# A pooling mixer rebuilt as projection first and banded products on TensorE, and the last expert routing table left in SBUF

## The chip, the cores and the metric

The kernel runs on one core of a Trainium2 chip. The metric is the device time of one execution in microseconds. The kernel before takes 3367.31 us, the median of three runs (3367.08 to 3372.91).

## What is computed

A residual block with depth 2 and then a second block, on 512 tokens (T) of 1024 channels (D), all in float32. Order of the work: feed-forward 0, pooling mixer, feed-forward 1 (layer 0); feed-forward 2, convolution mixer, feed-forward 3 (layer 1); then a mixer of attention and a linear recurrence, and a product-key expert layer (PEER) with 16384 single-neuron experts. The two parts that the change touches:

```python
def pool_mixer(h, w_grp, scale):          # windows 2, 4, 8, 16, one for each group of 256 channels
    cs = cumsum(hg, axis=1)
    pooled = (cs - lag(cs, w)) / min(pos, w)
    mixed = pooled - hg
    return einsum('btgc,gcd->btgd', mixed, w_grp) * scale

def peer_ffn(x, ...):                     # per token, 8 heads x 16 picks
    g = softmax(best_s); u = expert_u[idx]; v = expert_v[idx]
    return einsum('thk,thkd->td', g * gelu(einsum('td,thkd->thk', xc, u)), v)
```

The h that enters the pooling mixer is `x * rstd * coef + shift`, with rstd the inverse root of the mean square of a token over its channels, and coef and shift per channel from the conditioning vector c.

## The kernel before, in words

**Layout.** Activations are held transposed: channels on the 128 partitions, the 512 tokens along the free axis, in 8 tiles `x[:, k, :]` of 128x512. Every product is made in split precision: each operand is written as a high part (fp32r, made by ScalarE) and a low part (the rest, made by VectorE or GpSimd), and three matmuls (high by high, high by low, low by high) go into one PSUM bank (`three`, L1763).

**Weight stream.** One stream of 599 groups of 128x1024 weights (512 KB each) goes through a ring of R = 4 slots. SyncE loads a group into `raw` (L505) when the low part of the group four before is made; ScalarE makes `whi` (`hi`, L567 to L575) when TensorE has used the slot; GpSimd makes `wlo` (L532), and in the last two stages VectorE does (L1601). A semaphore carries each of these steps. All instructions of an engine are issued in the order of the program, so a waiting instruction holds up what stands behind it on its engine.

**Around the pooling mixer.** The output product of feed-forward 0 ends in four banks; VectorE adds each to x (L1262), ScalarE squares the tile (L594), VectorE sums the squares (L1096), and `mean_square` (L1836) takes the mean over the channels with a matmul by a constant matrix, so that each partition has the mean square of every token. Then come a root on ScalarE (L612) and a reciprocal of 128x512 on VectorE (`inverse_root`, L1113). The mixer itself, before: for each of 8 tiles VectorE multiplies by rstd (L1335), ScalarE applies scale and shift into a padded row (L701), VectorE makes the window sum by 1, 2, 3 or 4 shifted additions (`pool_mix`, L1314), corrects the first tokens (L1319), divides and subtracts (L1320), ScalarE makes the high part (L707), VectorE the low part (L1328), and only then can TensorE multiply by the group's weights: 48 matmuls of 512 columns (issued through `three`). VectorE adds the results to x (L1344). Eight `keep_busy` matmuls stand at the head of this stage on TensorE.

**Next stage.** Feed-forward 1 starts with `deferred_pair` (L1801): its first two weight groups are multiplied by `x * coef` not yet normed (`xs_hi` by `scaled_high`, L603; `xs_lo` by `scaled_low`, L1126), the norm is put on the result afterwards. Before, it first waits for the seventh tile of x; L1819 is its first matmul. `first_pair` (L1780) does groups three and four with the normed h.

**Expert layer, first pass ("up").** For each of 128 columns m of experts TensorE makes 24 matmuls of 384 columns (tokens 128 to 511), ScalarE applies gelu and stores the result (192 KB) to DRAM `expert_acts` (L930). Tokens 0 to 127 are done by gathered rows instead: GpSimd issues 128 indirect DMAs of 512 KB into a ring of 4 (L556), and VectorE takes a dot product of each (L1613). In between, 16 chunks for each of three blocks of 128 tokens (j = 0, 1, 2) are turned into a routing table `spread` (64 KB in each partition) by one-hot matmuls (L2142). After the chunks of a block its table is written to DRAM `expert_weights` in 8 pieces of 1 MB (L994) during the columns that follow: for j = 2 one piece per column from column 112 on. After these ScalarE issues the load of x back from DRAM (`x_back`, 2 MB, L998).

**Expert layer, second pass ("down").** For each m ScalarE loads one column of the tables (`g_ring`, 192 KB, L1013) and the stored gelu (`act_in`, 192 KB, L1014), three columns ahead; VectorE multiplies them (L1723), ScalarE makes the high part (L1025), VectorE the low part (L1727), and TensorE makes 18 matmuls of 512 columns (L2183 to L2185). For each m VectorE also adds one gathered row of v to the result of the first 128 tokens (L1735). VectorE still has nine dot products and four low parts of weights to make in order before and between the first of these steps. Before step 3 ScalarE waits until all gelu results are stored. After step 3 TensorE turns x_back by 64 small matmuls (L2165) and goes on.

## Time and profile before

| | before |
|---|---|
| median of 3 runs | 3367.31 us |
| profiled execution | 3378.14 us |
| its span | 3376.3 us |
| mean granted TensorE clock | 0.973 |
| TensorE matmul busy | 3223.0 us, 95% |
| VectorE busy | 2039.0 us, 60% |
| ScalarE busy | 1319.1 us, 39% |
| GpSimd busy | 1371.8 us, 41% |
| DMA | 636.91 MB |

The profile is one execution taken by the hardware profiler. Shares over the whole span say little for a change to two places; the sections of the span in which TensorE is not full are where time can be won. A granted clock of 1 is the level of 2.4 GHz, 0.5 that of 1.2 GHz. Times in brackets in a row of the time line are the idle time of the engine just before, with what ended it.

### The profile page before, as it was taken

Reading aid. Unit: us, or ns where it says so; the run is one execution under the profiler, and the core shown is the slowest. Engines: PE = TensorE matmul, PEld = TensorE weight load, DVE = VectorE, ACT = ScalarE, POOL = GpSimd, SP = SyncE. Lnnn points to the kernel's source line nnn. Section 1 sums busy time; section 2 is a strip of 40 time slices with the busy share of each in tenths; the row PEclk is TensorE's granted clock in tenths of the full one; section 3 lists DMA queues with packets and bytes.
Section 4 is the critical chain, followed back from the end, with each engine's and each line's share of the span. In section 5 each row is a group of like instructions: output and inputs, shape, how many; then the busy total and the mean of one; then the engine's idle time right before and its main releaser. Section 6 shows DMA issues by size and latency. Waiting matters only on the chain. (4 is left out here: it accounts for less than half of the span.)

```text
span 3376.3 us, 44805 instructions
## 1 busy us (share of the span) xinstructions
PE 3223.0 (95%) x15268; PEld 2753.7 (82%) x15268; DVE 2039.0 (60%) x2980; ACT 1319.1 (39%) x2029; POOL 1371.8 (41%) x686
## 2 busy tenths in 40 slices
PE   6999889999999999999998899999989897999999
PEld 4888668888888888888876677999989896888887
DVE  5562386613653164411157668987957766888887
ACT  3222243323332233322244653244857652333333
POOL 3444335444544444444443224466423343222221
PEclk8999989999999999999999889999999998999999
DMA  6554325532654222222322003355888899999997
GB/s 251 195 189 144 106 88 205 195 110 81 216 191 145 95 89 99 94 93 95 106 81 75 25 32 113 102 172 172 293 322 306 291 349 363 342 361 361 366 358 273
DMA packets 237531, 636.91 MB, mean 189 GB/s; under 512 B 22880, under 2 KB 105056, under 8 KB 233824
## 3 DMA queue, kind: packets, MB, share of 16 engines
q1 hardware_dynamic: 89440, 324.78, 27.5%
q10 hardware_dynamic: 111104, 176.30, 14.8%
q0 software_dynamic: 36864, 134.23, 11.2%
q8 instruction: 72, 1.18, 0.1%
q14 instruction: 51, 0.42, 0.0%
HBM read 580.69 MB, written 54.53 MB: 188 GB/s over the span
## 5 line engine op out<-in xcount | busy, mean ns | idle before, releaser
L532 POOL TENSOR_TENSOR wlo<-raw,whi 128x1024 fp32r<-128x1024 f32 x394 | 1022.4, 2598 | 1233.3 <-ACT whi L575 1232.7
L1765 PE MATMUL bank<-hhi,whi 128*128 128x512 f32 (+1 forms) x2688 | 1005.8, 374 | 51.4 <-DVE hlo L1328 22.1
L1766 PE MATMUL bank<-hlo,whi 128*128 128x512 f32 (+1 forms) x2688 | 997.2, 371 | 0.0
L1767 PE MATMUL bank<-hhi,wlo 128*128 128x512 f32 (+1 forms) x2688 | 996.6, 371 | 0.0
L575 ACT ACTIVATE whi<-raw 128x1024 fp32r<-128x1024 f32 x599 | 631.9, 1058 | 911.2 <-PE bank L1767 532.9
L1765 PEld LDWEIGHTS bank<-hhi,whi 128*128 128x128 f32 x2688 | 510.0, 190 | 123.8 <-issue 23.9
L1767 PEld LDWEIGHTS bank<-hhi,wlo 128*128 128x128 f32 x2688 | 509.4, 190 | 66.8
L1766 PEld LDWEIGHTS bank<-hlo,whi 128*128 128x128 f32 x2688 | 510.0, 190 | 66.1 <-issue 0.7
L1064 DVE CUSTOM_DVE_ANT_0 ada_raw<-ada_raw,cond_row 128x1024 f32<-128x1024 f32 x128 | 307.3, 2432 | 156.9 <-DMA ada_raw<-ada_dram 156.8
L1601 DVE TENSOR_TENSOR wlo<-raw,whi 128x1024 fp32r<-128x1024 f32 x205 | 250.7, 1223 | 161.8 <-ACT whi L575 140.2
L2183 PE MATMUL bank<-whi,we 128*128 128x512 f32 x768 | 300.4, 391 | 9.4 <-DVE we L1727 6.1
L556 POOL DMA_INDIRECT ring<-u_rows_dram,cell_u x128 | 179.2, 1400 | 298.0 <-DVE dots L1613 278.7
L2184 PE MATMUL bank<-whi,we 128*128 128x512 f32 x768 | 299.9, 390 | 0.0
L2185 PE MATMUL bank<-wlo,we 128*128 128x512 f32 x768 | 299.7, 390 | 0.0
L556 POOL DMA_INDIRECT ring<-stream_dram,cell_v x128 | 140.9, 1101 | 365.1 <-DVE y L1735 354.9
L1765 PE MATMUL bank<-uhi,whi 128*128 (+1 forms) x704 | 273.9, 389 | 0.0
L1766 PE MATMUL bank<-ulo,whi 128*128 (+1 forms) x704 | 273.9, 389 | 0.0
L1767 PE MATMUL bank<-uhi,wlo 128*128 (+1 forms) x704 | 273.9, 389 | 0.0
L644 ACT ACTIVATE uhi<-u 128x512 f32 (+1 forms) x88 | 55.6, 632 | 421.7 <-DVE u L1207 419.1
L1207 DVE TENSOR_TENSOR u<-silu,bank 128x512 f32<-128x512 f32 x85 | 58.2, 685 | 260.1 <-PE bank L1767 215.6
L2183 PEld LDWEIGHTS bank<-whi,we 128*128 128x128 f32 x768 | 144.8, 189 | 40.7 <-issue 4.9
L1613 DVE CUSTOM_DVE_ANT_0 ring<-ring,h_row 128x1024 f32<-128x1024 f32 x128 | 153.2, 1220 | 36.8 <-DMA ring<-u_rows_dram,cell_u 36.6
(326 smaller groups left out, 4063.6 us busy)
## 6 DMA issues: line engine op xcount, KB each, us to landing
raw<-stream_dram SPq DMA_DIRECT2D x599, 512.0 KB
ada_raw<-ada_dram ACTq DMA_DIRECT2D x128, 512.0 KB, 4.1
expert_acts<-act_out ACTq DMA_DIRECT2D x128, 192.0 KB
expert_weights<-spread ACTq DMA_DIRECT2D x24, 1024.0 KB
g_ring<-expert_weights ACTq DMA_DIRECT2D x128, 192.0 KB
act_in<-expert_acts ACTq DMA_DIRECT2D x128, 192.0 KB
first_raw<-ada_dram SPq DMA_DIRECT2D x8, 1024.0 KB, 18.1
x<-xin_dram ACTq DMA_DIRECT2D x1, 2048.0 KB, 7.1
```

The source lines that it names most:

```text
L532: pool.tensor_tensor(wlo[:, s, :, :], raw[:, s, :, :], whi[:, s, :, :].bitcast(F32), ALU.subtract).then_inc(lo_ready, 1)
L556: pool.indirect_dma_start(ring[:, q % RING, :], None, rows, bass.IndirectOffsetOnAxis(ap=cell[:, c:c + 1], axis=0)).then_inc(ring_landed[q ...
L575: act.activation(whi[:, s, :, :], raw[:, s, :, :], ACT.Copy).then_inc(hi_ready, 1)
L1064: dve.tensor_tensor_reduce(ada_raw[:, u % 2, :], ada_raw[:, u % 2, :], cond_row[:, :], 1.0, 0.0, ALU.mult, ALU.add, ada_dot[:, u % KT:u % ...
L1601: dve.tensor_tensor(wlo[:, s, :, :], raw[:, s, :, :], whi[:, s, :, :].bitcast(F32), ALU.subtract).then_inc(lo_ready, 1)
L1613: dve.tensor_tensor_reduce(ring[:, q % RING, :], ring[:, q % RING, :], h_row[:, :], 1.0, 0.0, ALU.mult, ALU.add, dots[:, q:q + 1]).then_in ...
L1765: pe.matmul(bank, whi[:, s, b, :], rhi, start=start, stop=False)
L1766: pe.matmul(bank, whi[:, s, b, :], rlo, start=False, stop=False)
L1767: return pe.matmul(bank, wlo[:, s, b, :], rhi, start=False, stop=stop)
L2183: pe.matmul(bank, we[:, m % WSLOTS, 0, toks], rh, start=m == 0, stop=False, skip_group_check=True)
L2184: pe.matmul(bank, we[:, m % WSLOTS, 1, toks], rh, start=False, stop=False, skip_group_check=True)
L2185: mm = pe.matmul(bank, we[:, m % WSLOTS, 0, toks], rl, start=False, stop=last, skip_group_check=True)
```

## The change

**Pooling mixer.** The mean over tokens and the multiplication by the group weights commute, and the factor rstd of a token can be put on after the weights. The new kernel multiplies `xs = x * coef` (made as for the deferred pairs, `scaled_high(1, k)` and `scaled_low(1, k)`, the first four tiles during feed-forward 0) by the weights with xs stationary and the weights moving, so that the result z has tokens on the partitions: `project`, 6 matmuls of 256 columns for each of 4 token tiles and 4 groups. The same product for the shift (`wide`, 24 matmuls) is made first and copied to SBUF by ScalarE. The mean square is made per token on a partition (four matmuls of two columns), so root and reciprocal are of 128x8. VectorE makes z = psum * rstd + wide_out (8 of 128x512), ScalarE rounds (8), VectorE makes the low parts (8). Pooling minus identity is then a product of z with constant banded matrices, 144 columns wide, 8 matmuls for each of 8 channel tiles and one more for the first tokens of windows 4, 8 and 16. The result lands in channel layout and VectorE adds it to x as before. The constants (576 KB) are loaded on ScalarE's queue during the output product of feed-forward 0; `pool_setup` and one rounding of 128x1152 on ScalarE prepare them there. `keep_busy(8)`, the padded rows and the DMA of `corr` go. The deferred pair of feed-forward 1 waits for the fourth tile of x instead of the seventh.

**Expert layer.** The table of block j = 2 stays in `spread` and is no longer written out or read back: `g_ring` loads shrink to 128 KB, VectorE's multiplication is two instructions (256 and 128 columns), and the wait for the last written pieces goes. Buffers move: `x_back` now lies where hhi was and is loaded after the last up column, ahead of the last store of `expert_acts` on the same queue.

The diff, cut to what the text speaks of:

```diff
...
+    bands_raw = place("bands_raw", 88, [P, 4, 2 * BAND], F32)
+    bands = place("bands", 187.5, [P, 4, 2 * BAND], F32R)
+    wide_hi = place("wide_hi", 195.5, [P, KT, P], F32R)
+    wide_lo = place("wide_lo", 199.5, [P, KT, P], F32R)
+    wide_out = place("wide_out", 139.5, [P, D], F32)
+    z32 = place("z32", 175.5, [P, 4, T], F32)
+    z_hi = place("z_hi", 107.5, [P, TT, D], F32R)
+    z_lo = place("z_lo", 123.5, [P, TT, D], F32R)
...
-    we = place("we", 100, [P, WSLOTS, 2, TD], F32R)
-    x_back = place("x_back", 116, [P, KT, T], F32)
-    y = place("y", 132, [P, TT, D], F32)
-
-
-    expert_weights = nc.dram_tensor("expert_weights", (DT, P, NK, P), F32).ap()
+    act_in = place("act_in", 181, [P, 4, TD], F32)
+    we32 = place("we32", 187, [P, 2, TD], F32)
+
+    we = [place(f"we{s}", at_kb, [P, 2, TD], F32R) for s, at_kb in enumerate((190, 193, 196, 172))]
+    x_back = place("x_back", 64, [P, KT, T], F32)
+    y = place("y", 80, [P, TT, D], F32)
...
+    expert_weights = nc.dram_tensor("expert_weights", (DT - 1, P, NK, P), F32).ap()
...
                     if q == 0:
                         for k in range(4):
                             ada_load(KT * LATE + 4 * half + k)
+                        if half == 0:
+                            act.dma_start(bands_raw[:, :, :], bands_in).then_inc(const_landed, 16)
+                        else:
+                            act.wait_ge(const_landed, 64)
+                            act.wait_ge(u_ready, FT)
+                            act.activation(bands[:, :, :], bands_raw[:, :, :], ACT.Copy).then_inc(bands_hi, 1)
                     with act.Fori(0, 2) as i:
                         for j in range(4):
                             hi(c + 1 + j, i, 4)
                     if half:
                         for k in range(4):
                             square(SUB_NORM[q] + 1, k)
-                            if q:
-                                scaled_high(7 if q == 3 else SUB_NORM[q] + 1, k)
+                            scaled_high(7 if q == 3 else SUB_NORM[q] + 1, k)
...
-            norm(1, pool_out, squared=4)
-            pool_round(KT - 1)
+            for k in range(4, KT):
+                square(1, k)
+                scaled_high(1, k)
+            act.wait_ge(pool_banks, 1)
+            for half in range(2):
+                act.activation(wide_out[:, half * T:(half + 1) * T], psum[6 + half][:, :], ACT.Copy).then_inc(wide_copied, 1)
+            act.wait_ge(ms_ready, ALL_NORMS.index(1))
+            act.activation(tok_std[:, :], psum[3][:, 0:2 * TT], ACT.Sqrt, bias=S("eps")).then_inc(std_ready, 1)
             hi(SEG["pool"][0] + LOOK)
-            hi(SEG["pool"][0] + LOOK + 1)
+            for half in range(2):
+                for tt in range(TT):
+                    act.wait_ge(pool_z, TT * half + tt + 1)
+                    act.activation(z_hi[:, tt, half * T:(half + 1) * T], z32[:, tt, :], ACT.Copy).then_inc(pool_hi, 1)
+                if half == 0:
+                    hi(SEG["pool"][0] + LOOK + 1)
             norm(2, h_high, ahead=SEG["ffn1_in"][0] + LOOK)
...
-                    pieces = (k,) if j == DT - 1 else (2 * k, 2 * k + 1)
-                    for p in pieces:
-                        if p < PIECES:
+                    for p in (2 * k, 2 * k + 1):
+                        if j < DT - 1 and p < PIECES:
                             rows = slice(PIECE * p, PIECE * p + PIECE)
-                            act.dma_start(expert_weights[j][:, rows, :], spread[:, rows, :]).then_inc(
-                                spilled if j < DT - 1 or p < PIECES // 2 else spilled_late, 16)
-                    if j == DT - 1 and k == PIECES:
-                        act.wait_ge(spilled, 16 * PIECES * (DT - 1) + 16 * PIECES // 2)
-                        act.dma_start(x_back[:, :, :], x_kept).then_inc(x_landed, 16)
+                            act.dma_start(expert_weights[j][:, rows, :], spread[:, rows, :]).then_inc(spilled, 16)
                     column(CHUNK_AT[j] + CHUNKS + k, None)
...
+            act.dma_start(x_back[:, :, :], x_kept).then_inc(x_landed, 16)
             store_acts(NK - 1, None)
             act.wait_ge(ring_used, PICKS)
             act.activation(gel[:, :], dots[:, :], ACT.Gelu_apprx_tanh).then_inc(gel_ready, 1)
-            act.wait_ge(spilled_late, 16 * PIECES // 2)
...
+            def pool_setup():
+
+                dve.wait_ge(bands_hi, 1)
+                for g in range(1, 4):
+                    w = 2 << g
+                    dve.tensor_tensor(corner_lo[:, CORNER[w]:CORNER[w] + w], bands_raw[:, g, 0:w], bands[:, g, 0:w].bitcast(F32),
+                                      ALU.subtract).then_inc(setup_done, 1)
+                shift = mod[:, 3 * KT:4 * KT].unsqueeze(2).to_broadcast([P, KT, P])
+                dve.wait_ge(ada_used, KT * (LATE + 1))
+                dve.tensor_copy(wide_hi[:, :, :], shift).then_inc(setup_done, 1)
+                dve.wait_ge(setup_done, 5)
+                dve.tensor_tensor(wide_lo[:, :, :], shift, wide_hi[:, :, :].bitcast(F32), ALU.subtract).then_inc(setup_done, 1)
...
+            def pool_low(q):
+                half, tt = q // TT, q % TT
+                dve.wait_ge(pool_hi, q + 1)
+                cols = slice(half * T, (half + 1) * T)
+                dve.tensor_tensor(z_lo[:, tt, cols], z32[:, tt, :], z_hi[:, tt, cols].bitcast(F32), ALU.subtract).then_inc(pool_ready, 1)
+
+            dve.wait_ge(std_ready, ALL_NORMS.index(1) + 1)
+            dve.reciprocal(tok_rstd[:, :], tok_std[:, :]).then_inc(rstd_ready, 1)
+            dve.wait_ge(rstd_ready, ALL_NORMS.index(1) + 1)
+            dve.wait_ge(wide_copied, 2)
+            for q in range(2 * TT):
+                half, tt = q // TT, q % TT
+                if tt < TT - 1:
+                    dve.wait_ge(pool_banks, 3 * half + tt + 2)
+                else:
+                    dve.wait_ge(pe_groups, SEG["pool"][0] + half + 1)
+                if q >= TT:
+                    dve.wait_ge(pool_ready, q - TT + 1)
+                dve.scalar_tensor_tensor(z32[:, tt, :], psum[4 - 4 * half + tt][:, :], tok_rstd[:, 2 * tt:2 * tt + 1],
+                                         wide_out[:, half * T:(half + 1) * T], ALU.mult, ALU.add).then_inc(pool_z, 1)
+                if q:
+                    pool_low(q - 1)
+            pool_low(2 * TT - 1)
+            for k in range(KT):
                 dve.wait_ge(pool_mixed, k + 1)
-                dve.tensor_tensor(hlo[:, k, :], mix32[:, k % 2, :], hhi[:, k, :].bitcast(F32), ALU.subtract).then_inc(pool_ready, 1)
-
-            inverse_root(1)
-            for k in range(KT + 1):
-                if k < KT:
-                    if k >= 2:
-                        dve.wait_ge(pool_h, k - 1)
-                    dve.tensor_tensor(xn[:, k % 2, :], x[:, k, :], rstd[:, :], ALU.mult).then_inc(xn_ready, 1)
-                if k:
-                    pool_mix(k - 1)
-            pool_low(KT - 1)
-            for k in range(KT):
-                if k % 4 == 3:
-                    dve.wait_ge(pe_groups, SEG["pool"][0] + k // 4 + 1)
-                else:
-                    dve.wait_ge(pool_banks, 3 * (k // 4) + k % 4 + 1)
-                dve.scalar_tensor_tensor(x[:, k, :], psum[k][:, :], coef[:, 1, KT + k:KT + k + 1], x[:, k, :],
+                dve.scalar_tensor_tensor(x[:, k, :], psum[(k + 4) % KT][:, :], coef[:, 1, KT + k:KT + k + 1], x[:, k, :],
                                          ALU.mult, ALU.add).then_inc(x_ready, 1)
...
-                dve.tensor_tensor(we32[:, m % 2, :], act_in[:, m % 4, :], g_ring[:, m % 4, :], ALU.mult).then_inc(we_mul, 1)
+                dve.tensor_tensor(we32[:, m % 2, 0:TD - P], act_in[:, m % 4, 0:TD - P], g_ring[:, m % 4, :], ALU.mult)
+                dve.tensor_tensor(we32[:, m % 2, TD - P:TD], act_in[:, m % 4, TD - P:TD], spread[:, m, :], ALU.mult).then_inc(we_mul, 1)
...
-                pe.wait_ge(x_ready, KT * (min(n, 8) - 1 - (n == 7)) + (7 if n in (2, 5, 10) else 4))
+                pe.wait_ge(x_ready, KT * (min(n, 8) - 1 - (n == 7)) + (7 if n in (5, 10) else 4))
...
-            keep_busy(8)
-            mean_square(1)
...
+            def project(out, g, hi, lo):
+
+                rows = pool_weights(g)
+                for k in range(2):
+                    pe.matmul(out, hi(2 * g + k), rows[k][0], start=k == 0, stop=False, skip_group_check=True)
+                    pe.matmul(out, hi(2 * g + k), rows[k][1], start=False, stop=False, skip_group_check=True)
+                for k in range(2):
+                    mm = pe.matmul(out, lo(2 * g + k), rows[k][0], start=False, stop=k == 1, skip_group_check=True)
+                return mm
+
+            pe.wait_ge(lo_ready, pool0 + 2)
+            pe.wait_ge(setup_done, 6)
+            pe.wait_ge(x_ready, 4)
             for g in range(4):
-                c = SEG["pool"][0] + g // 2
-                if g % 2 == 0:
-                    pe.wait_ge(lo_ready, c + 1)
-                pe.wait_ge(pool_ready, 2 * g + 2)
-                for o in range(2):
-                    for k in range(2):
-                        mm = three(psum[2 * g + o][:, :], c % R, (g % 2) * 4 + o * 2 + k, hhi[:, 2 * g + k, :], hlo[:, 2 * g + k, :],
-                                   k == 0, k == 1)
-                    mm.then_inc(pe_groups if g % 2 and o else pool_banks, 1)
+                mm = project(psum[6 + g // 2][:, 256 * (g % 2):256 * (g % 2) + 256], g,
+                             lambda k: wide_hi[:, k, :], lambda k: wide_lo[:, k, :])
+            mm.then_inc(pool_banks, 1)
+            for half in range(2):
+                pe.wait_ge(xs_hi_ready, scaled_before(1) + 4 * half + 4)
+                pe.wait_ge(xs_ready, scaled_before(1) + 4 * half + 4)
+                for tt in range(TT):
+                    if half == 0 and tt == 2:
+                        pe.wait_ge(wide_copied, 2)
+                        pe.wait_ge(sq_used, tiles_before(SQ_NORMS, 1) + KT)
+                        for m in range(TT):
+                            mm = pe.matmul(psum[3][:, 2 * m:2 * m + 2], sqsum[:, P * m:P * m + P], mean_d[:, 0:2], start=True, stop=True,
+                                           skip_group_check=True)
+                        mm.then_inc(ms_ready, 1)
+                    if half and tt == 3:
+                        pe.wait_ge(std_ready, ALL_NORMS.index(1) + 1)
+                    for g in (2 * half, 2 * half + 1):
+                        mm = project(psum[4 - 4 * half + tt][:, 256 * (g % 2):256 * (g % 2) + 256], g,
+                                     lambda k: xs_hi[1][:, k, P * tt:P * tt + P], lambda k: xs_lo[1][:, k, P * tt:P * tt + P])
+                    mm.then_inc(pool_banks if tt < TT - 1 else pe_groups, 1)
+            for half in range(2):
+                pe.wait_ge(pool_ready, TT * half + TT)
+                for k in range(4 * half, 4 * half + 4):
+                    g, w = k // 2, 2 << (k // 2)
+                    out, cols = psum[(k + 4) % KT], slice(P * k, P * k + P)
+                    for part in (z_hi, z_lo):
+                        first = part is z_hi
+                        for tt in range(TT):
+                            n = min(BAND, T - P * tt)
+                            at_col = 0 if tt == 0 else BAND
+                            mm = pe.matmul(out[:, P * tt:P * tt + n], part[:, tt, cols], bands[:, g, at_col:at_col + n],
+                                           start=first and tt == 0, stop=not first and tt == TT - 1, skip_group_check=True)
+                        if first and g:
+                            pe.matmul(out[:, 0:w], z_hi[:, 0, cols], corner_lo[:, CORNER[w]:CORNER[w] + w], start=False, stop=False, skip_group_check=True)
+                    mm.then_inc(pool_mixed, 1)
             ffn(1, KT)
...
```

## Rows read from the trace of the kernel before

**Rows 1.** The page: the span and each engine's busy time, share and instructions.
```profile
span 3376.3 us, 44805 instructions
...
PE 3223.0 (95%) x15268; PEld 2753.7 (82%) x15268; DVE 2039.0 (60%) x2980; ACT 1319.1 (39%) x2029; POOL 1371.8 (41%) x686
```

**Rows 2.** Windows: us, busy time of each engine, PEclk, DMA share, GB/s.
```profile
404.00:454.00 50.00, 21.16 (x67) 15.40 (x66) 46.38 (x76) 23.37 (x34) 4.92 (x2) 0.70 0.08 27
454.00:483.00 29.00, 29.00 (x133) 23.97 (x134) 24.61 (x35) 13.33 (x19) 8.17 (x2) 0.93 0.11 37
2739.00:2835.00 96.00, 74.47 (x388) 72.26 (x387) 54.95 (x79) 24.34 (x33) 39.01 (x31) 0.91 1.02 404
2835.00:2866.00 31.00, 26.20 (x133) 21.73 (x132) 21.43 (x33) 11.18 (x18) 6.98 (x5) 0.85 0.93 315
2866.00:3372.00 506.00, 506.00 (x2237) 419.07 (x2236) 413.70 (x489) 191.41 (x242) 135.62 (x124) 1.00 0.96 342
```

**Rows 3.** Time line of PE around the pooling mixer: start us, us, what.
```profile
403.42 0.39 PE L1767 MATMUL bank<-uhi,wlo 128*128 128x512 f32 x1
...
438.55 0.76 PE L1765 MATMUL bank<-hhi,whi 128*128 128x512 f32 x1 [6.23 <-DVE hlo L1328]
...
453.86 0.77 PE L1819 MATMUL bank<-xs_hi,whi 128*128 128x512 f32 x1 [6.72 <-issue]
```

**Rows 4.** Time line of DVE in the same stretch.
```profile
408.69 3.35 DVE L1113 RECIPROCAL rstd<-std 128x512 f32<-128x512 f32 x1 [1.49 <-ACT std L612]
...
443.47 1.40 DVE L1344 SCALAR_TENSOR_TENSOR x<-bank,coef,x 128x512 f32<-128x512 f32 x2
...
447.12 2.19 DVE L1096 TENSOR_TENSOR sqsum<-sqsum,sq 128x512 f32<-128x512 f32 x1
...
449.90 0.67 DVE L1096 TENSOR_TENSOR sqsum<-sqsum,sq 128x512 f32<-128x512 f32 x1
```

**Rows 5.** Time line of PE: matmuls of 256 columns in the attention stage.
```profile
1922.21 0.28 PE L2025 MATMUL bank<-w_lo,v_hi 128*128 128x256 f32 x1
1922.33 0.29 PE L2026 MATMUL bank<-w_hi,v_lo 128*128 128x256 f32 x1
```

**Rows 6.** Time line of PE: matmuls of 128 columns in the query stage.
```profile
2160.40 0.28 PE L2093 MATMUL bank<-key_hi,qt_hi 128*128 128x128 f32 x1
2160.51 0.27 PE L2094 MATMUL bank<-key_lo,qt_hi 128*128 128x128 f32 x1
```

**Rows 7.** Time line of PE at the turn from up to down.
```profile
2834.63 0.77 PE L2183 MATMUL bank<-whi,we 128*128 128x512 f32 x1 [4.61 <-DVE we L1727]
...
2840.79 0.79 PE L2183 MATMUL bank<-whi,we 128*128 128x512 f32 x1 [3.26 <-ACT act_out L938]
...
2855.10 0.47 PE L2183 MATMUL bank<-whi,we 128*128 128x512 f32 x1 [1.54 <-DVE we L1727]
```

**Rows 8.** DMA from 2739 to 2835 us: totals and issues by line.
```profile
DMA packets 12154, 38.79 MB, mean 404 GB/s; under 512 B 1235, under 2 KB 5204, under 8 KB 10998
...
expert_weights<-spread ACTq DMA_DIRECT2D x8, 1024.0 KB
...
x_back<-x_kept ACTq DMA_DIRECT2D x1, 2048.0 KB, 27.0
...
ring<-u_rows_dram,cell_u POOLq DMA_INDIRECT x31
```

**Rows 9.** The page: DMA issues, KB each, us to landing.
```profile
x<-xin_dram ACTq DMA_DIRECT2D x1, 2048.0 KB, 7.1
```

**Rows 10.** Time line of ACT: the wait for the stored gelu results.
```profile
2852.17 1.06 ACT L575 ACTIVATE whi<-raw 128x1024 fp32r<-128x1024 f32 x1 [5.35 <-DMA expert_acts<-act_out]
```

**Rows 11.** Time line of DVE: one step of the down pass, and act_w.
```profile
2854.87 0.28 DVE L1747 TENSOR_TENSOR act_w<-gel,gain 128x128 f32<-128x128 f32 x1
...
3201.04 0.55 DVE L1723 TENSOR_TENSOR we<-act_in,g_ring 128x384 f32<-128x384 f32 x1
3202.31 1.23 DVE L1601 TENSOR_TENSOR wlo<-raw,whi 128x1024 fp32r<-128x1024 f32 x1 [0.72 <-ACT whi L575]
```

129 lines of the change are left out of this document (49 added, 80 removed).

## Prediction

> **What bounds the kernel now.** I read the page first: TensorE (PE) is busy 95% of a span of 3376.3 us [rows 1], so only places where PE stands still or runs at the lower clock can give time. The windows show them [rows 2]. From 2866 to 3372 us, the down pass, PE is full at clock 1.00: 505.9 us for 124 steps, 4.08 us each. Nothing there can be won on another engine. Two places are not full. Around the pooling mixer, from the last matmul of feed-forward 0 at 403.42 to the first of feed-forward 1 at 453.86, 50.4 us pass [rows 3], PE is busy for under half of that and its clock averages well below 1 [rows 2]; the time line says that PE waits for VectorE (DVE), 6.23 us in the gap shown [rows 3], while DVE makes window sums without a pause. And from 2739 to 2866 us, the end of the up pass, PE is busy 74.5 of 96 us and 26.2 of 31 us, with the DMA engines at a share of 1.02 and 0.93 [rows 2]: there the bound is the transfers. 404 GB/s is what they reach with this mix [rows 8].
>
> **Pooling mixer, step by step.** The time line is redone from 403.65 us, when PE is free.
> PE, projections: 24 matmuls for the shift and 4 x 4 x 6 = 96 for xs, all of 256 columns. The nearest rows put such a matmul 0.12 us after the one before [rows 5], so 120 x 0.12 = 14.4 us, and about 0.9 us for the four mean-square matmuls of two columns (eight passes at the 0.11 us at which matmuls of 128 columns follow each other [rows 6]). PE ends its projections at 419.0. xs of tiles 0 to 3 is made 10 us earlier, beside the output product; the four more passes of ACT over a tile there push one weight rounding by under 3 us, which the ring of four slots covers; if it did not, PE would lose those 3 us.
> DVE and ACT beside it: squares are summed by about 406, xs_lo of the last four tiles by 408.6, wide_out is copied by 408.2 (two ACT copies of about 0.6 us after the first 24 matmuls end at 406.5), the mean square is there at about 410.1, root and reciprocal are now of eight columns, some 0.6 us together instead of 3.35 us for the reciprocal alone [rows 4]. From 410.8 DVE makes eight times z (0.66 us, as two readings of a bank took 1.40 in [rows 4]) and its low part (0.6 us, as the 0.67 us addition there): 10.1 us, to about 421. In it falls GpSimd's making of two weight low parts; beside such a piece of work one addition of two SBUF tiles took 2.19 us instead of 0.67 [rows 4], so I add 1.5 us for each: 424. The bound below is no such loss, 421.
> The Trainium skill says of this ("GPSIMD Engine Reference", Key points) that GpSimd shares its SBUF interfaces with VectorE and contends with instructions that have two SBUF inputs. By that the low parts are hit and the z, with one input in PSUM, are not, and the trace agrees: 2.19 against 0.67 us.
> PE, bands: 8 x 8 matmuls of at most 144 columns and 6 corners, 70 x 0.112 = 7.8 us. The first half can run at once from 419.0 to 422.8; the second waits for DVE at 424 and ends at 428.
> DVE then needs 1.26 us per tile of x (0.66 and 0.6 for the sum of squares), so the fourth tile is there at about 428.2, and the deferred pair, which no longer waits for the seventh, starts there. That is 25.7 us before 453.86 [rows 3].
> After that: before, the window from 454 to 483 ran at a mean clock of 0.93 [rows 2], which is 29 x 0.07 = 2.0 us; with PE not idle for more than about 2 us at a time it should start at full clock. Against this stands the mean square in the middle of the deferred pair, which needs all eight tiles: PE gets there at about 434, the last sum at 434.8, 0.9 us. Gain of this part: 25.7 + 2.2 - 0.9 = 27 us. Its ends: 30 (no contention at all) and 20 (each hand-over between PE, ACT and DVE 0.3 us dearer over some 24 of them).
> For narrow matmuls the Trainium skill ("TensorE: Matmul & The Clock Gate", Back-to-back issue gap) gives 81 ns as the sustained spacing at 128 columns. The trace has 0.11 us here, weight load included [rows 6], and the sum goes by that; by the page's figure the bands would take 5.7 us instead of 7.8, an estimate, most of it hidden behind DVE.
>
> **Start.** One small DMA less stands ahead of the weight loads on SyncE: between 0 and 0.5 us, taken as 0.3.
>
> **Expert table, up pass.** Removed between 2739 and 2835 us: eight writes of 1 MB, 8.39 MB, the load of x back, 2.10 MB, and 64 KB of each of five loads of the tables, 0.33 MB: 10.8 of 38.8 MB [rows 8]. The 28.0 MB that stay need 69 us at 404 GB/s. PE alone needs 16 columns x 24 matmuls x 0.1735 us = 66.6 us. DVE needs 36 gathered rows in this stretch; 31 came in 96 us before, 3.1 us each [rows 8], beside the large writes. The queues do not interlock perfectly, since DVE takes rows and weights in one order, so I take 76 to 77 instead of 69 us: 96 - 77 = 19 us won. Ends: 26 (only the bytes count) and 10 (the gathers stay at 2.4 us each, 36 x 2.4 = 86).
>
> **Expert table, turn to down.** What was hidden before is now in the way: x_back is issued only after the last up column, and the last store of the gelu results stands behind its 2 MB on the same queue. ACT waits for that store before step 3, and with it wait the rounding and low part of the weights of step 3 and all later loads of tables. Before, that wait was 5.35 us [rows 10] and cost PE 1.54 us [rows 7]. A load of the same size took 7.1 us at the start of the kernel [rows 9] and 27.0 us when it came behind the writes [rows 8]. In the new place little else is in its queue, so it is nearest to 7.1 to 9 us: the store lands 4 to 7 us later, PE waits 5 us more. Ends: 2 and 20 us. PE itself needs x_back only after 16.3 us of its own steps.
> The Trainium skill ("DMA: Bandwidth & Descriptors", Queues, rings and completion order) says that a DMA engine goes round between queues by packets and takes one ring in order. By that the store cannot pass x_back, which is the cost just named; no row of before shows that order.
>
> **Down pass.** DVE's one multiplication of 0.55 us [rows 11] becomes one of 256 and one of 128 columns, about 0.42 and 0.28 us (the latter as act_w [rows 11]); issued back to back they cost some 0.07 to 0.15 us more. DVE stands idle 0.72 us in each step [rows 11], so that hides them and the cost is nothing; without that idle time it would be 124 x 0.1 = 12 us. Table loads of 128 instead of 192 KB free DMA time that PE does not wait for: 0.
>
> **Sum.** 27 + 0.3 + 19 - 5 = 41.3 us. The profiled execution took 3378.14 us, 10.8 more than the median of 3367.31. Against its own time: 3336.8. Taken from the median: 3326.0 us, if the parts are as large without the profiler. The 10.8 us may well lie in the stretch that is bound by DMA; then its gain is smaller in the timed runs by up to that.
>
> **Rivals.**
> (a) The turn eats the second part: x_back is slow again, near the 27.0 us of [rows 8]; the store comes 20 us late, and the 19 us are given back, or the gathers stay the bound and little was won. For it: share 1.02 in the stretch [rows 2] and four gathers in flight at the turn. Against it: the 8 MB that stood before it in its queue are gone. Time: 3367.3 - 27 = 3340.
> (b) The change does not do on PE what it says: the projections run at the lower clock, 1.2 GHz, at which 256 columns take 0.213 us, as [rows 3] show 6.23 us gaps before a slow start, and DVE's chain, not PE, sets the pace with each hand-over. 120 x (0.213 - 0.12) = 11 us less: 3337. Against it: PE is full from 403.65 on, and the gaps foreseen are under 2 us.
> The Trainium skill ("TensorE: Matmul & The Clock Gate", HAM oscillation) warns of thin matmuls with waits between them, after which the clock falls again and again; by that this rival is the outcome. The waits on the trace that went with a fall here are of 6 us and more [rows 3].
> (c) Both parts reach their upper ends, 30 and 26 - 2: 3313.
> (d) Slower than before: in the down pass the pair of multiplications costs more than the row it replaces plus DVE's idle time, 0.47 + 0.72 = 1.19 us per step; from there each 0.1 us costs 124 x 0.1 = 12.4 us, and it needs 1.6 us a step to make the kernel slower by 7 us (41 + 7 = 48 us over 124 steps). For it: two instructions in place of one and the contention of [rows 4], where one took 1.5 us more. Against it: GpSimd computes nothing there. Time: 3375.
>
> **How the numbers follow.** Forecast 0.58, (a) 0.19, (b) 0.12, (c) 0.07, (d) 0.04. The forecast's case spans 3316 to 3337 by the bounds of its terms; with (a) and (b) and the doubt over the profiler's 10.8 us the range is 3314 to 3345. A measurement of this kernel can tell some 0.2%, 6.7 us, from no change. All cases but (d) are faster by more; I leave 0.01 for no change.
>
> **What would show it.** PE's first matmul of the deferred pair about 25 us after the last of feed-forward 0, instead of 50.4, with the granted clock 1.00 through the stage; z starting at about 411 and ending at 421 to 424; PE with at most two waits of 1 to 2 us. The first matmul of the down pass 77 us after the last chunk (96 before), no issue to expert_weights for the third block, x_back landing in 7 to 10 us, and a PE wait of 5 to 8 us before step 3. The forecast is wrong if PE shows waits in the steady down pass, if the clock falls between 404 and 430, or if the stretch from 2739 stays above 86 us.

## The result and the profile after

The changed kernel takes 3338.1 us (median of 4 runs, 3336.3 to 3339.6); the kernel before, run beside it and earlier, 3368.7 us. The ratio is 0.9896, 95% interval 0.9884 to 0.9908. So the change gives 30.6 us, where 41.3 were forecast, and the time is 12.1 us above the forecast of 3326.0. 3338.1 lies in the range of 3314 to 3345, but just outside the 3316 to 3337 that the terms of the sum allowed by themselves. The profiled execution took 3338.93 us, with a span of 3337.1 us, 39.2 less than the span of before [rows 1]. So the two traces differ by 8.6 us more than the medians do, and part of what is laid out below is a difference between executions.

The windows of after, at the stages of [rows 2] (us, busy time of each engine with the number of instructions, granted clock, DMA share, GB/s):

```profile
412.00:420.00 8.00, 8.00 (x71) 8.00 (x69) 8.00 (x10) 3.36 (x5) 3.24 (x2) 1.00 0.22 68
420.00:428.00 8.00, 6.25 (x37) 6.12 (x36) 7.82 (x13) 5.30 (x10) 0.00 (x0) 0.65 0.18 66
428.00:436.00 8.00, 8.00 (x30) 7.13 (x30) 7.89 (x13) 5.39 (x9) 0.00 (x0) 0.50 0.01 2
...
2709.00:2787.00 78.00, 68.15 (x389) 67.00 (x388) 54.65 (x80) 24.02 (x33) 40.88 (x31) 0.98 0.97 362
2787.00:2827.00 40.00, 29.48 (x134) 24.09 (x134) 21.89 (x41) 11.38 (x18) 6.53 (x5) 0.78 0.85 294
2827.00:3337.00 510.00, 506.37 (x2236) 419.01 (x2235) 422.25 (x609) 191.96 (x243) 143.28 (x124) 1.00 0.92 326
```

PE (TensorE) is full from 404 to 420 us and again from 428, where before it was busy 21 of 50 us. But the clock falls in the window from 420 to 428 us (0.65) and is 0.50 in the next. The up-pass stretch is 78 us long instead of 96; the turn behind it is longer, 40 us instead of 31, with a clock of 0.78 instead of 0.85; the down pass is as full as before but for the last 4 us of the span.

The time line of PE around the pooling mixer, which answers to [rows 3] (last matmul of feed-forward 0, first band product, the second half of the bands, first matmul of the deferred pair, first matmul on hhi):

```profile
402.16 0.39 PE L1763 MATMUL bank<-uhi,wlo 128*128 128x512 f32 x1
...
417.67 0.56 PE L1949 MATMUL bank<-bands,z_hi 128*128 128x144 f32 x4
...
423.32 1.12 PE L1949 MATMUL bank<-bands,z_hi 128*128 128x144 f32 x4 [1.75 <-DVE z_lo L1317]
...
431.06 0.73 PE L1815 MATMUL bank<-xs_hi,whi 128*128 128x512 f32 x1
...
448.91 0.48 PE L1783 MATMUL bank<-hhi,whi 128*128 128x512 f32 x1
```

The deferred pair starts 28.9 us after feed-forward 0, against 50.4 before. There is one wait of 1.75 us, for DVE's last low parts. In front of it 32 band products and two corners took 3.9 us (417.67 to the wait's begin at 421.57, 0.11 us each); behind it 32 and four take 7.7 us (423.32 to 431.06, 0.21 each).

DVE and GpSimd in the same stretch, which answers to [rows 4]:

```profile
407.77 0.17 DVE L1122 CAST shifts<-mod 128x8 fp32r<-128x8 f32 x1
...
409.67 1.41 DVE L1331 SCALAR_TENSOR_TENSOR z<-bank,tok_rstd,wide_out 128x512 f32<-128x512 f32 x2
...
410.42 2.41 POOL L537 TENSOR_TENSOR wlo<-raw,whi 128x1024 fp32r<-128x1024 f32 x1 [9.67 <-ACT whi L580]
...
411.12 2.25 DVE L1317 TENSOR_TENSOR z_lo<-z,z_hi 128x512 fp32r<-128x512 f32 x1
...
413.96 0.68 DVE L1317 TENSOR_TENSOR z_lo<-z,z_hi 128x512 fp32r<-128x512 f32 x1
...
417.74 2.21 DVE L1317 TENSOR_TENSOR z_lo<-z,z_hi 128x512 fp32r<-128x512 f32 x1
...
423.18 1.40 DVE L1338 SCALAR_TENSOR_TENSOR x<-bank,coef,x 128x512 f32<-128x512 f32 x2
...
440.94 3.35 DVE L1116 RECIPROCAL rstd<-std 128x512 f32<-128x512 f32 x1 [2.09 <-ACT std L617]
```

The first row is a cast of eight columns, to be met again below. The long reciprocal is gone, z starts at 409.67, and the two low parts that meet GpSimd's work take 2.25 and 2.21 us, the others 0.68. Then DVE goes on to the x updates without a pause; it stands idle 2.09 us ahead of the reciprocal of the next norm, at 440.94.

The turn, which answers to [rows 7] and [rows 10]: two of PE's waits, then ACT's issue of x_back, the store behind it and the wait for that store:

```profile
2786.55 0.77 PE L2223 MATMUL bank<-whi,we 128*128 128x512 f32 x1 [6.21 <-DVE we L1722]
...
2813.62 0.77 PE L2223 MATMUL bank<-whi,we 128*128 128x512 f32 x1 [7.19 <-DVE we L1722]
```
```profile
2797.62 0.33 ACTq L1038 DMA_DIRECT2D x_back<-x_kept  x1
2797.99 0.44 ACTq L938 DMA_DIRECT2D expert_acts<-act_out  x1
...
2810.69 1.06 ACT L580 ACTIVATE whi<-raw 128x1024 fp32r<-128x1024 f32 x1 [11.90 <-DMA expert_acts<-act_out]
```

ACT is idle 11.90 us for the store, against 5.35, and PE waits 7.19 us for the weights of step 3, against 1.54.

One table serves for all that follows. It cuts each profiled span at the starts of the same six instructions: the last matmul of feed-forward 0 (A), the first of the deferred pair (B), the first matmul on hhi behind it (C), DVE's first reciprocal of qstd, at the start of the attention stage (D), the first of PE's last sixteen matmuls for hot_n, at the last chunk of the up pass (E), the first matmul of the down pass (F). All numbers are us.

| kernel | to A | A to B | B to C | C to D | D to E | E to F | F to end |
|---|---|---|---|---|---|---|---|
| before | 403.4 | 50.4 | 17.6 | 1288.3 | 977.6 | 97.3 | 541.7 |
| after | 402.2 | 28.9 | 17.9 | 1288.2 | 970.3 | 79.1 | 550.5 |

The start gives 1.2 us, the pool stage (A to C) 21.3, the up pass (E to F) 18.2, and the turn (in F to end) takes 8.8 back. A fifth item stands in no step of the prediction: 7.3 us between D and E, where the change touches nothing. Together they are the 39.2 us, but for rounding.

### The profile page after: what moved, and what is told of

It is laid out like the page before. It is cut to its first block and busy times, and to the rows that moved or that the text cites. A ratio compares the mean times of both kernels' runs of the same rounds, so it can differ in the third digit from the quotient of the medians.

```text
span 3337.1 us, 45156 instructions
## 1 busy us (share of the span) xinstructions
PE 3215.9 (96%) x15400; PEld 2753.1 (82%) x15400; DVE 2035.5 (61%) x3084; ACT 1317.3 (39%) x2032; POOL 1376.2 (41%) x686
## 5 line engine op out<-in xcount | busy, mean ns | idle before, releaser
L1761 PE MATMUL bank<-hhi,whi 128*128 128x512 f32 (+1 forms) x2672 | 992.8, 372 | 16.0 <-DVE qn L1417 11.1
L1763 PE MATMUL bank<-hhi,wlo 128*128 128x512 f32 (+1 forms) x2672 | 985.6, 369 | 0.0
L1762 PE MATMUL bank<-hlo,whi 128*128 128x512 f32 (+1 forms) x2672 | 985.6, 369 | 0.0
L1762 PEld LDWEIGHTS bank<-hlo,whi 128*128 128x128 f32 x2672 | 503.2, 188 | 64.7 <-issue 0.7
L561 POOL DMA_INDIRECT ring<-stream_dram,cell_v x128 | 148.1, 1157 | 366.9 <-DVE y L1730 356.8
L2225 PEld LDWEIGHTS bank<-wlo,we 128*128 128x128 f32 x768 | 145.6, 190 | 30.6
## 6 DMA issues: line engine op xcount, KB each, us to landing
first_raw<-ada_dram SPq DMA_DIRECT2D x8, 1024.0 KB, 18.2
```

The source lines that it names most:

```text
L561: pool.indirect_dma_start(ring[:, q % RING, :], None, rows, bass.IndirectOffsetOnAxis(ap=cell[:, c:c + 1], axis=0)).then_inc(ring_landed[q ...
L1761: pe.matmul(bank, whi[:, s, b, :], rhi, start=start, stop=False)
L1762: pe.matmul(bank, whi[:, s, b, :], rlo, start=False, stop=False)
L1763: return pe.matmul(bank, wlo[:, s, b, :], rhi, start=False, stop=stop)
L2225: mm = pe.matmul(bank, we[m % WSLOTS][:, 0, toks], rl, start=False, stop=last, skip_group_check=True)
```

## Experiments

Twelve runs follow, in three groups of four; after_again and xback_again repeat a kernel. The runs of one group share a chip and their runs of the kernel before. With the traces of before and after that makes fourteen traces.

| kernel | median us | before, same group | ratio, 95% interval |
|---|---|---|---|
| pool_only | 3346.8 | 3372.6 | 0.9921 (0.9907 to 0.9935) |
| table_only | 3367.3 | 3372.6 | 0.9981 (0.9972 to 0.9990) |
| xback_after_store | 3329.5 | 3372.6 | 0.9872 (0.9857 to 0.9887) |
| after_again | 3338.5 | 3372.6 | 0.9894 (0.9879 to 0.9910) |
| gap_wide | 3339.2 | 3374.9 | 0.9898 (0.9881 to 0.9914) |
| gap_narrow | 3338.4 | 3374.9 | 0.9893 (0.9876 to 0.9909) |
| wide_among_bands | 3339.9 | 3374.9 | 0.9894 (0.9878 to 0.9911) |
| pad_100 | 3363.7 | 3374.9 | 0.9964 (0.9950 to 0.9978) |
| xback_again | 3327.6 | 3373.1 | 0.9871 (0.9854 to 0.9887) |
| split_early | 3327.3 | 3373.1 | 0.9869 (0.9852 to 0.9885) |
| split_early_fill | 3328.4 | 3373.1 | 0.9873 (0.9853 to 0.9893) |
| both_filled | 3333.4 | 3373.1 | 0.9882 (0.9866 to 0.9899) |

Their profiled spans, cut as above:

| kernel | to A | A to B | B to C | C to D | D to E | E to F | F to end |
|---|---|---|---|---|---|---|---|
| pool_only | 402.3 | 28.9 | 17.9 | 1288.2 | 969.7 | 98.8 | 542.3 |
| table_only | 402.9 | 50.5 | 17.3 | 1288.3 | 977.3 | 77.9 | 551.0 |
| xback_after_store | 402.8 | 28.9 | 18.2 | 1288.2 | 967.7 | 79.5 | 541.9 |
| after_again | 402.0 | 27.2 | 18.3 | 1288.3 | 967.7 | 80.4 | 551.6 |
| gap_wide | 402.0 | 25.2 | 18.5 | 1289.5 | 974.4 | 77.9 | 550.1 |
| gap_narrow | 402.7 | 25.2 | 18.5 | 1289.5 | 972.6 | 78.8 | 551.0 |
| wide_among_bands | 402.1 | 25.2 | 18.5 | 1291.1 | 972.6 | 79.0 | 551.0 |
| pad_100 | 402.5 | 50.9 | 17.3 | 1288.3 | 972.9 | 79.5 | 550.7 |
| xback_again | 402.4 | 28.9 | 17.9 | 1288.0 | 967.7 | 79.9 | 541.3 |
| split_early | 402.1 | 28.0 | 18.2 | 1288.3 | 966.9 | 79.3 | 541.3 |
| split_early_fill | 402.0 | 26.4 | 20.7 | 1288.1 | 972.2 | 78.2 | 541.1 |
| both_filled | 402.4 | 25.2 | 18.5 | 1289.8 | 975.2 | 79.5 | 541.3 |

### The two halves alone: pool_only, table_only, after_again

pool_only leaves the routing table as in the kernel before (its last block is stored and loaded back, x_back comes behind the writes, one multiplication per step). table_only keeps the old window sums. after_again is after, unchanged. The cores of the edits:

```diff
# pool_only keeps, of the table part of the change, the lines of before:
 act.dma_start(expert_weights[j][:, rows, :], spread[:, rows, :]) ...   # for all three blocks
 if j == DT - 1 and k == PIECES: ... act.dma_start(x_back[:, :, :], x_kept) ...
 dve.tensor_tensor(we32[:, m % 2, :], act_in[:, m % 4, :], g_ring[:, m % 4, :], ALU.mult)
# table_only keeps, of the pool part, the lines of before:
 norm(1, pool_out, squared=4) ... pool_mix(k) ... three(psum[2 * g + o][:, :], ...)
```

> Only the pool part of the change; the routing table is stored and loaded back as in the kernel before. My theory: the parts are independent, and the pool part is worth what the two traces show between the last matmul of the first feed-forward and the deferred pair, 50.4 - 28.9 = 21.5 us, plus about 1 us at the start: 22 us under the kernel before, about 3346 us. The granted clock falls to 0.50 in the bands again, and the up-pass stretch before the turn is 96 us long again and the turn 31 us. Rival: the bands and the table part disturb each other, or the whole gain is elsewhere, for instance in the clock of later stages: then this kernel is either over 3352 (less than 17 us) or under 3341 us.

> Only the table part of the change (last table kept in SBUF, x_back moved, the multiplication split); the pooling is as in the kernel before. My theory: 18 us from the up pass, 9 us given back at the turn: 9 us under the kernel before, about 3360 us, with a stretch before the turn of 77 us and a turn of 40 us. Rival: the table part is worth its full 18 us and the pool part only 13, the 9 us at the turn being variation: about 3350 us, turn 32 us. Second rival: the table part is worth nothing, over 3366 us. The start is 1.3 us earlier in the after kernel; if that is from the pool part's dropped load, this kernel has its last matmul of the first feed-forward at 403.4 us as before.

> The after kernel unchanged, as the yardstick of the three others in the same rounds: 3338 us, 30.6 under before. My theory has it at the sum of the two halves to within 2 us; a rival, that the halves interact, has it off their sum by 4 us or more.

Measured: pool_only is 25.8 us under before (22 expected), table_only 5.3 (9 expected), their sum 31.1, and after in the same rounds 34.1. The intervals, 3 to 5 us to each side, leave no sign that the halves interact: the 2.9 us between sum and whole lie between the 2 of the theory and the 4 of the rival. The cut spans are sharper. pool_only has the A to B of after to 0.1 us, with the clock at 0.50 again, and the long up pass and short turn of before (641.1 us from E to the end, before 639.0); table_only has A to D of before, 77.9 us from E to F (19.4 less) and 551.0 behind F (9.3 more). So the up pass gained what was expected of it, and the turn gave back half. The first rival for table_only, that the turn's loss is variation, falls: its turn is long as well. The second, that this part is worth nothing and the time over 3366 us, is met in its number (3367.3) only because before itself is slower in this group; taken against the runs beside it, 3367.3 us is a gain clear of noise.

But the median of table_only shows 5.3 us (3 to 9 by its interval) where its trace shows 10 from E to the end. One thing blurs such comparisons, and it can be read from the record of every run: the time of one and the same kernel goes with its mean granted clock. The thirty runs of before in the three groups span 12 us. The six at a clock of 0.972 or 0.973 took 3375.1 to 3378.8 us, the nine at 0.977 or 0.978 took 3366.8 to 3373.3; each group by itself shows the same order. The profiled execution of before has 0.973 and 3378.1. The part of the 5 us that is such variation was not separated from the rest.

The start does not decide between the halves: A lies between 402.0 and 402.9 us in all twelve, 0.5 to 1.4 before the one profiled execution of the kernel before.

### The turn: xback_after_store, xback_again

```diff
-            act.dma_start(x_back[:, :, :], x_kept).then_inc(x_landed, 16)
             store_acts(NK - 1, None)
+            act.dma_start(x_back[:, :, :], x_kept).then_inc(x_landed, 16)
```

> The after kernel with the load of x_back issued behind the store of the last activation column instead of ahead of it, nothing else. My theory: the 2 MB load ahead of the store in ACT's queue is what makes the load of activations behind it late, so ScalarE's idle time before the split in the turn falls from 11.9 us to about 5.4, the PE wait of 7.19 us for we falls to about 1.5, and the kernel is 5 to 6 us faster than after, 3332 to 3333 us (36 us under before). x_back itself then lands before it is used, since the turn of x starts 22 us after its issue. Rival: the wait comes from something else (the earlier end of the up pass, or the gathered rows on the other queue): PE's wait stays at about 7 us and the time at 3338. Second rival: x_back lands too late and the turn of x waits for it: 3338 or more.

> The kernel with x_back loaded behind the last store once more, as the yardstick of the next three: 9 us under after, about 3330 us; 46 to 47 us from the last matmul of feed-forward 0 to the first on hhi, and 966 to 972 us from the first reciprocal of qstd to the last chunk of the up pass.

Measured: 3329.5 us against 3338.5 for after in the same rounds, 9.1 us faster where 5 to 6 were expected, and 3327.6 in another group. The time line of ACT in xback_after_store, with the store, x_back behind it and the wait, then the time line of PE with the wait for step 3 and the turn of x:

```profile
2796.46 0.35 ACTq L938 DMA_DIRECT2D expert_acts<-act_out  x1
2796.84 0.67 ACTq L1039 DMA_DIRECT2D x_back<-x_kept  x1
...
2802.99 1.06 ACT L580 ACTIVATE whi<-raw 128x1024 fp32r<-128x1024 f32 x1 [5.12 <-DMA expert_acts<-act_out]
```
```profile
2805.93 0.47 PE L2223 MATMUL bank<-whi,we 128*128 128x512 f32 x1 [1.12 <-DVE we L1722]
...
2810.14 7.30 PE L2205 MATMUL bank<-sq_plain,x_back 128*128 128x128 f32 x64
```

ACT is idle 5.12 us instead of 11.90, PE waits 1.12 us instead of 7.19. The wait came from the 2 MB ahead of the store, as the first theory had it; the transfer itself took 11.8 us here and 11.1 in after, from issue to landing (10.9 in xback_again), and nobody waits for it: PE comes to the turn of x at 2810.14 us, 13.3 after the issue at 2796.84, and starts it without a wait. The gain is larger than PE's wait. Two windows from the first matmul of the down pass, in after and in xback_after_store, show the rest (columns as in the windows above; cut at the start of step 3):

```profile
2786.50:2813.60 27.10, 16.55 (x54) 12.54 (x55) 12.73 (x24) 5.78 (x10) 6.53 (x5) 0.75 0.84 300
2813.60:2820.00 6.40, 6.38 (x18) 5.07 (x19) 6.40 (x13) 3.46 (x5) 0.00 (x0) 0.61 0.90 274
```
```profile
2785.30:2805.90 20.60, 15.79 (x54) 11.89 (x55) 12.84 (x24) 5.73 (x10) 6.17 (x5) 0.75 0.99 366
2805.90:2812.00 6.10, 6.07 (x35) 5.35 (x36) 6.10 (x13) 4.00 (x6) 0.00 (x0) 1.00 1.02 369
```

The steps before the wait take 27.1 us against 20.6, 6.5 more; behind the long wait the clock is 0.61 for 6.4 us, behind the short one it is 1.00, and that is 2.5 us. Together 9.0, and F to end is 8.6 shorter. This is the version that beats both kernels.

### The bands: gap_wide, gap_narrow, wide_among_bands

The clock falls to 0.50 behind the wait between the two halves of the bands in all kernels that have the pool part as it is (0.65, then 0.50 in the windows of after; 0.81, then 0.55 in after_again, where it falls later). Three theories: PE's standstill makes the clock fall (A), the narrow products do (B), or what ran before 418 us does (C). The edit of gap_wide; gap_narrow has fifteen matmuls of 144 columns instead, wide_among_bands two of 512 in the gap and two behind each of the first three groups of the first half:

```diff
             for half in range(2):
+                if half:
+                    pe.wait_ge(pool_z, 5)
+                    for _ in range(7):
+                        pe.matmul(psum[0][:, :], xs_hi[1][:, 0, 0:P], xs_hi[1][:, 0, :], start=True, stop=True, ...)
                 pe.wait_ge(pool_ready, TT * half + TT)
```

> The after kernel with seven extra matmuls of 512 columns (7 x 0.227 = 1.6 us, their results are overwritten) between the first and the second half of the band products, where PE stood still for 1.75 us. Theory A: the standstill makes the clock fall. Then the bands run at 1.00 to their end (0.112 us each), the deferred pair starts 25 instead of 28.9 us after the last matmul of feed-forward 0 and itself runs at full clock: 5 to 6 us faster than after, 3333 us. Theory B: the narrow bands (144 columns, before and after the gap) make it fall, gap or no gap: clock 0.50 again from about 422 us, 28 to 29 us, 3338. Theory C: the fall is set by what ran before 418 us (projections of 256 columns): also as B, but then neither this run nor one with wide matmuls among the bands changes it.

> The after kernel with fifteen extra matmuls of 144 columns (15 x 0.112 = 1.7 us, results overwritten) in the same gap. Theory A (standstill): full clock, 25 us from feed-forward 0 to the deferred pair, 3333 us. Theory B (narrow bands): clock 0.50 from about 422 us as in after, 28 to 29 us or more, 3338 to 3340 us.

> The after kernel with two matmuls of 512 columns behind each of the first three band groups of the first half and two in the gap (8 x 0.227 = 1.8 us in all, results overwritten). Theory B (narrow bands): the clock stays at 1.00 through the stage, the deferred pair starts at 25 to 26 us, 3333 us. Theory A: about the same, since the gap is filled to 0.3 us. Theory C: the clock falls all the same at about 422 us, 29 to 30 us, 3339. Together with the two runs with only the gap filled it tells the three apart.

Windows of gap_wide (the last one belongs to what is said below), then one of gap_narrow:

```profile
420.00:428.00 8.00, 7.93 (x60) 7.14 (x60) 7.81 (x13) 5.45 (x10) 0.00 (x0) 1.00 0.19 66
428.00:436.00 8.00, 7.63 (x38) 6.11 (x37) 7.89 (x14) 6.64 (x11) 0.00 (x0) 1.00 0.01 2
...
445.00:449.00 4.00, 3.21 (x8) 2.55 (x9) 4.00 (x7) 4.00 (x7) 0.00 (x0) 0.62 0.00 0
```
```profile
420.00:428.00 8.00, 7.93 (x72) 7.79 (x71) 7.81 (x13) 4.72 (x9) 0.00 (x0) 1.00 0.19 66
```

In all three the clock is 1.00 from 404 to 444 us, and the deferred pair starts 25.2 us after feed-forward 0. Theory A holds, B and C fall: matmuls of 144 columns keep the clock as well as wide ones, as long as PE does not stand still. Whether a standstill of this length would also drop it behind wide matmuls was not tried.

But no time is won: the ratios to before are 0.9898, 0.9893 and 0.9894, against 0.9894 for after_again, and the times 3339.2, 3338.4 and 3339.9 us instead of the 3333 expected. The price that each theory put on the clock was wrong. The table shows where it goes. At C, 3.0 of the 3.7 us are left; from C to D it takes 1.3 us more (2.9 in wide_among_bands); from D to E 2 to 4 more than the 970.3 of after, 5 to 7 more than the 967.7 of after_again. The first of these steps is seen on the time lines of gap_wide, PE first, then DVE, then GpSimd, with one row of DVE in after at the end:

```profile
433.46 1.13 PE L1834 MATMUL bank<-sqsum,mean_d 128*128 128x512 f32 x2 [0.37 <-DVE sqsum L1099]
...
445.79 0.59 PE L1783 MATMUL bank<-hhi,whi 128*128 128x512 f32 x1 [2.33 <-ACT hhi L627]
```
```profile
423.04 1.40 DVE L1338 SCALAR_TENSOR_TENSOR x<-bank,coef,x 128x512 f32<-128x512 f32 x2
...
433.32 7.51 DVE L1129 SCALAR_TENSOR_TENSOR xs_lo<-x,coef,xs_hi 128x512 fp32r<-128x512 f32 x8
440.76 3.34 DVE L1116 RECIPROCAL rstd<-std 128x512 f32<-128x512 f32 x1
444.14 5.39 DVE L1149 SCALAR_TENSOR_TENSOR h<-x,coef,rstd 128x512 f32<-128x512 f32 x8
```
```profile
436.33 2.63 POOL L537 TENSOR_TENSOR wlo<-raw,whi 128x1024 fp32r<-128x1024 f32 x1 [17.07 <-ACT whi L580]
```
```profile
433.46 5.38 DVE L1129 SCALAR_TENSOR_TENSOR xs_lo<-x,coef,xs_hi 128x512 fp32r<-128x512 f32 x8
```

DVE works without a pause from the x updates at 423.04 over the low parts of xs to the reciprocal at 440.76 and h at 444.14. PE, now faster, waits 0.37 us for the last square sum and 2.33 us for the first hhi, and behind this wait the clock falls again (0.62 from 445 to 449; C to D is 1.3 us longer). In after, PE at half clock came to the same place at 448.91 without any wait, and it was DVE that stood idle. So DVE's chain is the next bound of this stage, 3.1 us behind PE's (448.91 - 445.79).

Of this chain, 2.1 us are one more collision with GpSimd. The eight low parts of xs take 7.51 us here and 5.38 in after, because GpSimd's weight low part comes at 436.3 to 437.1 us in all four traces with the gap filled, among them, and at 441.93 in after, behind them; the one it meets takes 2.88 us instead of 0.74. The root for the reciprocal was ready at 435.31, so by estimate DVE would have come to it 2.1 us earlier without that, which is most of PE's wait of 2.33. No run took this collision away.

### DVE's chain and GpSimd: split_early, split_early_fill, both_filled

Two of DVE's low parts of z take 2.2 us beside GpSimd. split_early moves one of the two weight splits ahead, to where ScalarE waits for the mean squares; all three contain the later x_back, and only both_filled has the collision just described.

```diff
+            hi(SEG["pool"][0] + LOOK)
             act.wait_ge(ms_ready, ALL_NORMS.index(1))
             act.activation(tok_std[:, :], psum[3][:, 0:2 * TT], ACT.Sqrt, bias=S("eps")).then_inc(std_ready, 1)
-            hi(SEG["pool"][0] + LOOK)
```

split_early_fill adds ten matmuls of 512 columns behind the deferred pair; both_filled has those ten and the seven of gap_wide, with the split where it was.

> As xback_again, and the split of one weight chunk (ScalarE's whi, then GpSimd's wlo, 2.4 us) issued ahead of ScalarE's std of the tokens instead of behind it, so that GpSimd works at 407.6 to 410.0 us and not beside the first z_lo. Theory D (DVE's chain sets the end of this stage, and the two z_lo of 2.2 us instead of 0.67 are 3 us of it): the first z_lo takes 0.7 us, the PE wait between the bands' halves falls from 1.75 to 0.2 us, the granted clock stays at 1.00, and from the last matmul of feed-forward 0 to the first on hhi it is 43.8 (as with the gap filled) - 1.6 = 42.2 us instead of 47: 3 to 5 us faster than xback_again if the attention stage takes the same time. Theory E (PE's own work sets it): 43.8 us or more. Rival: the collision only moves (xs_lo or z waits for GpSimd instead), DVE's z ends at 423.2 as before and nothing is won.

> As split_early, and ten extra matmuls of 512 columns (2.3 us, results overwritten) behind the deferred pair, where PE stood still 2.3 us for hhi once the bands ran at full clock, and where the clock then fell for some us. Theory: the stretch from the first matmul on hhi to the first reciprocal of qstd is 1288.2 us and not 1289.5 as with the bands' gap alone filled, so 1 us faster than split_early, or level with it if DVE is late by less than the filling takes. Rival: the fall there has another cause and the filling only costs up to 2 us.

> As xback_again, with both standstills of PE filled with matmuls of 512 columns (seven between the bands' halves, ten behind the deferred pair) and the split where it was. Theory D: 43.8 us to the first matmul on hhi (DVE's chain unchanged), then 1288.2 us: 3 to 4 us faster than xback_again where the attention stage takes the same time, 1.6 us slower than split_early_fill. Rival (the clock gives back later what it is spared here): the attention stage takes 4 to 5 us more, as in the three runs with a filled gap (973 to 974 us and more, against 968 to 970), and the time is that of xback_again.

DVE and GpSimd in split_early:

```profile
407.55 2.41 POOL L537 TENSOR_TENSOR wlo<-raw,whi 128x1024 fp32r<-128x1024 f32 x1 [6.81 <-ACT whi L580]
...
407.75 2.23 DVE L1122 CAST shifts<-mod 128x8 fp32r<-128x8 f32 x1
...
410.34 1.41 DVE L1331 SCALAR_TENSOR_TENSOR z<-bank,tok_rstd,wide_out 128x512 f32<-128x512 f32 x2
...
411.79 0.69 DVE L1317 TENSOR_TENSOR z_lo<-z,z_hi 128x512 fp32r<-128x512 f32 x1
...
422.31 1.40 DVE L1338 SCALAR_TENSOR_TENSOR x<-bank,coef,x 128x512 f32<-128x512 f32 x2
```

The rival holds: the collision only moves. The first z_lo now takes 0.69 us (the later one still 2.24), but a cast of 128x8 elements, which takes 0.17 us in after, takes 2.23: it ends at 409.98, and GpSimd's operation at 409.96. z starts at 410.34 instead of 409.67 and ends 0.9 us earlier instead of 1.6. PE's wait shrinks from 1.75 to 0.89 us, and that is still enough:

```profile
420.00:428.00 8.00, 7.11 (x40) 6.97 (x40) 7.82 (x13) 5.95 (x11) 0.00 (x0) 0.65 0.15 58
```

The clock is 0.65 here and 0.50 in the next 8 us, as in after, and the 42.2 us from A to C were missed by 4: 46.3. The time, 3327.3 us, is not told apart from the 3327.6 of xback_again. Theory D against E was not decided by this run, since the chain was shortened by 0.9 and not by 1.6 us and PE ran at half clock.

The fillings brought nothing either. In split_early_fill the clock fell later (0.76 from 420 to 428) behind the same wait of 0.89 us, C came at 47.1 us, since the ten matmuls were in the way, and the time is 3328.4. In both_filled the first part went as foreseen, 43.8 us to C, but C to D is 1289.8, not 1288.2 (the clock stayed at 1.00 there; PE's waits for GpSimd's low parts add up to 2.2 us between C and D instead of the 1.0 of xback_again, the rest was not found), and D to E 975.2, 7.5 more than in xback_again where the rival had said 4 to 5: 3333.4 us, 5.7 slower than xback_again. The rival had the direction right and the size too low. In none of these runs does what the clock is spared around the pooling mixer come through to the end.

### The 7 us behind the change: pad_100

Between D and E the instructions are the same in all fourteen traces, yet the stretch takes 966.9 to 977.6 us. pad_100 brings the later work back to the times it had before:

```diff
             pe.wait_ge(x_ready, 4)
+            pe.wait_ge(xs_hi_ready, scaled_before(1) + 1)
+            for _ in range(100):
+                pe.matmul(psum[7][:, :], xs_hi[1][:, 0, 0:P], xs_hi[1][:, 0, :], start=True, stop=True, ...)
             for g in range(4):
                 mm = project(psum[6 + g // 2]...
```

> The after kernel with a hundred extra matmuls of 512 columns (22.7 us, results overwritten) ahead of the projections, so that all later work comes at about the times it had in the kernel before. Theory P: between the deferred pair and the last chunk of the up pass, 2276 us in after and 2283 in before, the work is the same and only the times at which the clock falls in the attention stage differ, since everything starts 22.6 us earlier; so here the stretch is 2283 us again and the whole 3338 + 22.7 + 7 = 3368 us, less 2 to 5 where the clock no longer falls in the bands. Rival: the 7 us come from what the pool part changed itself (memory places, the queues' state), and not from the time of day: 2276 us again, 3361 us, less the same.

Measured: 3363.7 us, and 972.9 us from D to E (2278.5 from B to E, where theory and rival had named 2283 and 2276). Neither is met. The clock falls behind the bands' wait here too (0.61 from 451 to 459 us), so nothing comes off the theory's 3368 us or the rival's 3361, and the time lies between them. The first 340 us behind D, in before, in pad_100 and in after_again, show where the difference sits:

```profile
1759.79:2099.79 340.00, 297.73 (x1257) 233.80 (x1256) 258.50 (x474) 177.35 (x319) 116.93 (x66) 0.87 0.17 61
```
```profile
1759.03:2099.03 340.00, 295.07 (x1272) 230.71 (x1270) 263.34 (x493) 177.09 (x319) 117.53 (x66) 0.89 0.18 62
```
```profile
1735.81:2075.81 340.00, 294.43 (x1303) 230.50 (x1301) 268.22 (x519) 178.32 (x321) 119.92 (x67) 0.92 0.18 63
```

The clock is 0.87, 0.89 and 0.92 over the same work, and it goes with the time from D to E: over the fourteen traces from 0.92 (966.9 to 968 us) over 0.91 (970), 0.90 (972.2 to 974.4) and 0.89 (972.9) to 0.88 (975.2) and 0.87 (977.3 and 977.6). In this stage PE waits for DVE and ScalarE over and over, and how often the clock falls there differs from trace to trace. Some traces of nearly the same kernel are close (970.3 and 969.7 in after and pool_only, 977.6 and 977.3 in before and table_only), but after and after_again, one kernel, are 2.6 us apart (970.3 and 967.7), and the thirty runs of before, with their 12 us and clocks of 0.972 to 0.978, show that one kernel can vary by as much as these kernels differ. All six kernels with extra matmuls lie at 972.2 us or above, all six traces that have the new pooling without them at 970.3 or below; with one trace each, that is a pattern and not shown. Why is open. It is not the time at which the stage is reached: pad_100 and table_only come to D at 1759.0 both, and lie 4.4 us apart.

## Why the prediction was right and wrong

**Projections, z, contention: right.** The projections went as costed, 402.39 to 417.67 us, without a wait and at clock 1.00. z began at 409.67 and the low parts ended at 423.3, against 410.8 and 424, with the two collisions in it. What the Trainium skill says ("GPSIMD Engine Reference", Key points) of instructions with two SBUF inputs agrees with the z_lo. In split_early a cast of 128x8, with one input, waited as long. The same line of that page also names DVE's 2-port perf mode; no view here shows whether the cast ran in it.

**Bands: the spacing right, the clock wrong.** 0.11 us for a product, as taken from [rows 6], holds for the first half. The step that failed is "with PE not idle for more than about 2 us at a time it should start at full clock": a wait of 1.75 us, which the same sum had foreseen, was enough for the fall, and 0.89 us in split_early. The three runs with the gap filled give the 25.2 us of A to B, to 0.4 us the forecast of 24.8 (50.4 - 25.7 = 24.7). By the prediction's own words it is wrong if the clock falls between 404 and 430; it did. The kernel before could have warned of it: the prediction read only falls behind waits of 6 us and more, but in the attention stage of the same trace the clock is 0.50 from 1940 to 1948 us, right behind a wait of 1.42:

```profile
1938.62 0.50 PE L2024 MATMUL bank<-w_hi,v_hi 128*128 128x512 f32 x1 [1.42 <-POOL w_lo L548]
```
```profile
1940.00:1948.00 8.00, 8.00 (x28) 6.33 (x27) 3.61 (x9) 3.60 (x11) 1.13 (x2) 0.50 0.01 2
```

Rival (b) had the right kind of mechanism in the wrong place, the projections, and put too much on it: 11 us, where the bands cost 3.0 at C and nothing in the whole. That its 3337 us are nearest to the measured time is luck. The section HAM oscillation of "TensorE: Matmul & The Clock Gate", in the Trainium skill, which rival (b) quoted, describes a fall behind waits for DMA of 3 to 5 us between bursts of matmuls; thin there is said of the whole product, not of a narrow matmul. Here 1.75 us were enough, and the measurement decides.

**The 27 us of the pool part: 21.3 measured at C.** Of the missing 5.7, 3.0 are the clock (24.3 us from A to C with the gap filled). Another 0.5 is the start of the deferred pair, 25.2 us behind feed-forward 0 and not 24.7. The last 2.2 are a term that the sum had with the wrong sign: +2.2 for a deferred pair at full clock, less 0.9 for the mean square, is +1.3, and B to C with the gap filled measured -0.9 (18.5 us against 17.6). The text before the sum works the +2.2 out as 2.0. At full clock this pair ends early and PE waits 0.37 us for the sum and 2.33 us for hhi, since DVE still has the low parts of xs, the reciprocal and h to make, and one of those low parts meets GpSimd. The sum ended at the first matmul of the deferred pair; it should have followed DVE to the next place at which PE needs it. For the same reason the clock's fall cost less than it looked: filling the gap saved 3.0 us at C and nothing in the whole.

**Up pass: right.** 19 us forecast, 18.2 and 19.4 measured on the traces of after and table_only. The DMA totals of after from 2709 to 2787 us answer to [rows 8]:

```profile
DMA packets 10447, 28.25 MB, mean 362 GB/s; under 512 B 1100, under 2 KB 4620, under 8 KB 10444
```

28.25 MB, as counted, but at 362 GB/s, not 404, with the DMA engines still at a share of 0.97 in the window shown at the top. What is left has the smaller packets (2.7 KB in the mean against 3.2); whether that is the reason was not tested. The choice of 77 us over 69 was the right one. Its ground was in part wrong: 31 gathered rows came in this stretch, as in before, and not 36, at 2.5 us each instead of 3.1.

**Turn: the mechanism right, the term mis-sized.** -5 us were taken, 8.8 measured. ACT's wait grew by 6.55 us, in the range of 4 to 7, PE's step 3 came 6.5 us later, and the 2.5 us of low clock behind the longer wait were not in the sum. x_back took 11.1 us to land where 7 to 10 were expected. That the store does not pass the load was concluded from what the Trainium skill ("DMA: Bandwidth & Descriptors", Queues, rings and completion order) says, that an engine takes the entries of one ring in order; the traces agree: 5.12 us of idle time with the store first, 11.90 with it second. Rival (a), whose 3340 us are 1.9 from the measured time, is not what happened: it had the whole 19 us lost, and by the traces 9 to 10 of them stayed (5.3 by the median of table_only).

**Down pass: right.** DVE's pair of multiplications takes 0.42 and 0.28 us, and DVE still has some 0.65 us of idle time in a step, against 0.72 [rows 11]:

```profile
3149.63 0.42 DVE L1717 TENSOR_TENSOR we<-act_in,g_ring 128x256 f32<-128x256 f32 x1
3149.97 0.28 DVE L1718 TENSOR_TENSOR we<-act_in,spread 128x128 f32<-128x128 f32 x1
3150.90 1.23 DVE L1595 TENSOR_TENSOR wlo<-raw,whi 128x1024 fp32r<-128x1024 f32 x1 [0.65 <-ACT whi L580]
```

PE has no wait there. Rival (d) falls.

**The account.** 41.3 - 5.7 (pool) - 0.8 (up pass) - 3.8 (turn) + 0.9 (start) + 7.3 (D to E) = 39.2 us, the difference of the two spans. The medians give 8.6 less, since the profiled execution of before lay 9.4 us above its median (3378.1 against 3368.7) and that of after 0.8 above its own. The prediction had said that this excess may lie in the stretch bound by DMA and be missing from the gain. The runs of before point another way: their time goes with their mean granted clock, and the profiled execution, at 0.973, is one of the low ones. Where in the kernel the faster runs keep their clock is not known, since one trace of before was kept. So the sum missed two things that nearly cancel, one in the attention stage and one in the reference it was made against, and both may be the same variation of the clock; the error of 10.7 us (41.3 - 30.6) is, in size, that of the pool part and the turn. That 3338.1 us still lies in the stated range owes something to luck: the terms by themselves allowed up to 3337, and it was widened to 3345 for the rivals and for the profiler's 10.8 us.

## What to carry to other kernels

Follow a gain past the end of the stage that is changed, engine by engine, to the next place where the engine that was relieved needs the other one: here the freed engine met a chain about 3 us behind, and in the runs with the gap filled its earlier work moved a piece of GpSimd's into that chain, which made it 2 us longer. A large load put into a queue ahead of a small store delays the store: here ScalarE's wait for the store was 11.90 us with a load of 11 us ahead of it, and 5.12 with the load behind it. If someone waits for the store and nobody for the load, the order of two lines can be worth much, here 9 us. And a wait that costs 1 to 2 us by itself must be priced with the work at half clock behind it, but only up to where another engine takes over as the bound. Before a gain of a few us is read from two single traces, compare the mean granted clock of the runs: here the times of one kernel spread over 12 us along with it.

## What the runs showed of the hardware that was not expected

- A PE standstill of 1.75 us behind narrow products (144 columns), and one of 0.89 us in split_early, was followed by the lower clock in the second half of the bands; in before one of 1.42 us was. With the gap of 1.75 us filled by matmuls of 144 or of 512 columns the granted clock stayed at 1.00.
- What DVE's low parts and casts lose to GpSimd's operation on two SBUF tiles does not go by their size: the cast of 128x8 ended with it (2.23 us instead of 0.17), the low parts of 128x512 ended 0.5 us after it (2.25 instead of 0.68), while z, with one input in PSUM, ran beside it at its usual 0.7 us.
- The same instructions from D to E took 966.9 to 977.6 us, with a mean clock of 0.92 to 0.87 in the first 340 us of the attention stage. The cause was not found; thirty runs of one kernel, before, spread over 12 us, the slower the lower their mean granted clock (0.978 to 0.972). A comparison of two single traces can be off by as much.
